# The halves of a PSUM bank added by one reduction on VectorE, without ScalarE's copy

## What is computed

```python
h = rmsnorm(x, g_mix);  z = h @ w_in             # gates, conv inputs, q, k, v
conv_branch = (cb * causal_dwconv(cc * cv, conv_w)) @ w_conv_out
attn_branch = forgetting_attention(q, k, v, log_f) @ w_attn_out
x = x + (sigmoid(gate_c) * conv_branch + sigmoid(gate_a) * attn_branch) @ w_mix_out
x = x + square(relu(rmsnorm(x, g_mlp) @ w_ff1)) @ w_ff2          # width 8192
x = rmsnorm(x, g_final)
mod = silu(c) @ w_ada + b_ada                                     # second block
# attention and a state-space mixer on (norm(x) * (1 + scale) + shift) @ w_in_2
x = x + gate1 * (mixed @ w_out)
u = causal_dwconv(norm(x) @ w_up)                                 # width 2 * 5632
x = x + gate2 * ((silu(u_g) * u_v) @ w_down)
out = rms_norm(x, final_norm_g)
```

## Time and profile before

| | us |
|---|---|
| median of three runs (lowest, highest) | 2615.51 (2613.37, 2620.49) |
| the profiled execution, its own time | 2620.42 |
| its span, first to last instruction | 2618.6 |
| TensorE busy (mean granted clock 0.989) | 2549.9 |
| VectorE busy | 2032.7 |
| ScalarE busy | 1324.8 |

### The profile page before, as it was taken

How to read it: one execution, slowest core, us unless ns; L and a number is a source line. 1 busy time by engine, 2 the same in 40 slices (tenths; PEclk the granted TensorE clock), 3 DMA queues, 4 the chain that set the end, 5 groups by cost and what they waited for, 6 DMA issues and landing times.

```text
span 2618.6 us, 47653 instructions
## 1 busy us (share of the span) xinstructions
PE 2549.9 (97%) x14448; PEld 2211.2 (84%) x14448; DVE 2032.7 (78%) x3152; ACT 1324.8 (51%) x2048; POOL 5.2 (0%) x13
## 2 busy tenths in 40 slices
PE   8999999999999999999998999989899999999998
PEld 7888888888888888888887888868788888888886
DVE  7778775589887887887888558676888888888888
ACT  5444434565554454544554347544545545545456
POOL 0000000000000000000000000000000000000000
PEclk9999999999999999999999999999999999999999
DMA  7786873557888888888885554415455656556554
GB/s 278 258 278 205 269 246 132 182 184 258 278 282 278 279 283 281 279 283 278 281 279 189 175 174 155 138 55 184 146 189 171 200 181 182 191 176 192 191 164 157
DMA packets 160688, 561.95 MB, mean 215 GB/s; under 512 B 18131, under 2 KB 18428, under 8 KB 160636
## 3 DMA queue, kind: packets, MB, share of 16 engines
q1 hardware_dynamic: 132428, 459.04, 52.9%
q10 hardware_dynamic: 27792, 101.20, 12.0%
q0 software_dynamic: 416, 1.06, 0.2%
HBM read 559.12 MB, written 2.11 MB: 214 GB/s over the span
## 4 chain that ended last, share of the span: by engine, by line
PE 94%; DVE 3%; ACT 1%; issue 1%; DMA 1%; DVEq 0%; ACTq 0%; SPq 0%
PE bank L284 94%; DVE w_lo L973 1%; ACT w_hi L573 0%; DMA w_raw<-in_w_gate 0%; DVE R L1006 0%; PE bank L424 0%; DMA X<-in_x 0%; DVE Z L1056 0%; PE bank L415 0%; DVE ss L1423 0%; DVE Z L1577 0%; DVE G L1460 0%; DVE H L1438 0%; ACT scratch L592 0%; ACT bank L599 0%
## 5 line engine op out<-in xcount | busy, mean ns | idle before, releaser
L284 PE MATMUL bank<-H,w_hi 128*128 128x512 f32 (+1 forms) x4736 | 1658.9, 396 | 25.4 <-DVE w_lo L1024 9.9
L284 PE MATMUL bank<-H,w_lo 128*128 128x256 f32 x4672 | 1314.1, 282 | 0.0
L973 DVE TENSOR_TENSOR w_lo<-w_raw,w_hi 128x1024 fp32r<-128x1024 f32 x900 | 1092.2, 1222 | 144.4 <-ACT w_hi L573 136.2
L284 PEld LDWEIGHTS bank<-H,w_hi 128*128 128x128 f32 x4736 | 892.1, 189 | 234.0 <-issue 17.9
L573 ACT ACTIVATE w_hi<-w_raw 128x1024 fp32r<-128x1024 f32 x900 | 910.6, 1051 | 2.9 <-DMA w_raw<-in_w_gate 2.6
L284 PEld LDWEIGHTS bank<-H,w_lo 128*128 128x128 f32 x4672 | 889.5, 190 | 0.1
L284 PE MATMUL bank<-U,w_hi 128*128 128x512 f32 x1984 | 700.5, 397 | 5.5 <-DVE U L1558 4.9
L284 PE MATMUL bank<-U,w_lo 128*128 128x256 f32 x1984 | 558.0, 281 | 0.0
L592 ACT ACTIVATE scratch<-bank 128x256 f32<-128x256 f32 x356 | 136.8, 384 | 825.6 <-PE bank L284 825.5
L284 PEld LDWEIGHTS bank<-U,w_hi 128*128 128x128 f32 x1984 | 372.4, 188 | 98.0 <-DVE U L1558 6.2
L284 PEld LDWEIGHTS bank<-U,w_lo 128*128 128x128 f32 x1984 | 373.9, 188 | 0.0
(11 more groups left out here) (198 smaller groups left out, 1157.6 us busy)
## 6 DMA issues: line engine op xcount, KB each, us to landing
w_raw<-in_w_ff SPq DMA_DIRECT2D x256, 512.0 KB, 4.9
ada_w<-in_w_ada ACTq DMA_DIRECT2D x192, 512.0 KB, 4.6
w_raw<-in_w_up SPq DMA_DIRECT2D x176, 512.0 KB, 4.1
w_raw<-in_w_z SPq DMA_DIRECT2D x96, 512.0 KB, 4.8
w_raw<-in_w_in SPq DMA_DIRECT2D x88, 512.0 KB, 3.9
w_raw<-in_w_gate SPq DMA_DIRECT2D x64, 512.0 KB, 4.6
w_raw<-in_w_down SPq DMA_DIRECT2D x64, 384.0 KB, 3.1
w_raw<-in_w_down SPq DMA_DIRECT2D x64, 320.0 KB, 3.4
```

Of the source, the lines that this page charges most:

```text
L284: return nc.tensor.matmul(out, lhsT, rhs, start=start, stop=stop, skip_group_check=True)
L973: TT(w_lo[:, slot, :], w_raw[:, slot, :], w_hi[:, slot, :].bitcast(F32), ALU.subtract)\
```

## The change

A unit's sum is one `tensor_reduce` on VectorE that reads the whole bank as 256 groups of two, each group a column of the lower half and the column 256 further on, and adds each group. ScalarE's copies, their waits and `halves`, `halves_b`, `half` and `half2` are gone. VectorE waits for `piece_used` itself. In all units that have a `split_low` of slot 0, it now stands ahead of the sum on VectorE; `cast_high` of slot 0 comes first on ScalarE, where the copy was. In out2 and down the gate is applied in the instruction that adds to X. All other instructions are as before.

```diff
-            def take_half(pair, par, scale=1.0):
-
-                act.wait_ge(sem("piece_used"), CREDIT + 4 * pair + 2 * par + 2)
-                A(half[par], bank[par][:, T:2 * T], ACT.Copy, scale=scale).then_inc(sem("halves"), 1)
...
-            def add_halves(pair, par, out):
-
-                dve.wait_ge(sem("halves"), units_with_half(pair, par))
-                TT(out, bank[par][:, 0:T], half[par], ALU.add).then_inc(sem("bank_read"), 1)
+            def add_halves(pair, par, out, first=0):
+
+                dve.wait_ge(sem("piece_used"), CREDIT + 4 * pair + 2 * par + 2)
+                return v.tensor_reduce(out, bank[first + par][:, :].rearrange("p (a t) -> p t a", a=2), AX_X, ALU.add)
+
+            def add_unit(pair, par, out):
+
+                add_halves(pair, par, out).then_inc(sem("bank_read"), 1)
                 return 2 + 2 * pair + par + 1
...
                     pair, m = PAIR0["branch"] + i, 2 * i + par
-                    dve.wait_ge(sem("halves_b"), 2 * m + 2)
-                    TT(total[par], bank[par][:, 0:T], half[par], ALU.add).then_inc(sem("branch.sum"), 1)
-                    TT(conv[par], bank[2 + par][:, 0:T], half2[par], ALU.add).then_inc(sem("bank_read"), 1)
                     split_low(pair + 1, par, 0)
+                    add_halves(pair, par, total[par]).then_inc(sem("branch.sum"), 1)
+                    add_halves(pair, par, conv[par], 2).then_inc(sem("bank_read"), 1)
...
                         add_ada(ADA0["ff"] + 32 * g + u, int(g > 0), par)
-                        n = add_halves(pair + i, par, total[par])
+                        split_low(pair + i + 1, par, 0)
+                        n = add_unit(pair + i, par, total[par])
                         dve.wait_ge(sem("bank_read"), n)
 
                         STT(wide[par], total[par], 0.0, R[:, :], ALU.max, ALU.mult).then_inc(sem("ff.relu"), 1)
-                        split_low(pair + i + 1, par, 0)
                         dve.wait_ge(sem("ff.u_full"), m + 1)
                         TT(ob(U, u, 1), conv[par], ob(U, u, 0).bitcast(F32), ALU.subtract).then_inc(sem("ff.u_ready"), 1)
                         split_low(pair + i + 1, par, 1)
...
-                dve.wait_ge(sem("halves"), units_with_half(pair, par))
-                STT(total[par], bank[par][:, 0:T], mod[:, bass.ds(gate + block, 1)], half[par], ALU.mult, ALU.add)\
-                    .then_inc(sem("bank_read"), 1)
...
+                n = add_unit(pair, par, total[par])
+                dve.wait_ge(sem("bank_read"), n)
+                STT(xb(block), total[par], mod[:, bass.ds(gate + block, 1)], xb(block), ALU.mult, ALU.add)\
+                    .then_inc(sem(name + ".x"), 1)
...
-                    n = add_halves(pair + i, 0, total[0])
                     split_low(pair + i + 1, 0, 0)
+                    n = add_unit(pair + i, 0, total[0])
...
-                    n = add_halves(pair + i, 1, total[1])
+                    split_low(pair + i + 1, 1, 0)
+                    n = add_unit(pair + i, 1, total[1])
                     ffn_conv(pair + i, 1, m + 1, n)
                     dve.wait_ge(sem("up.silu"), j + 1)
                     dve.wait_ge(sem("up.conv"), m + 2)
                     TT(wide[0], wide[1], conv[1], ALU.mult).then_inc(sem("up.act"), 1)
-                    split_low(pair + i + 1, 1, 0)
```

More of the change, by code:

```diff
@@ L796, in ff2_unit @@
             def ff2_unit(pair, par, m, block, chunk, squares=False, last=False):
-                if last:
-                    cast_high(pair + 1, par, 0)
-                take_half(pair, par)
+                cast_high(pair + 1, par, 0)
                 if not last:
-                    cast_high(pair + 1, par, 0)
                     cast_high(pair + 1, par, 1)
@@ L900, in gated_unit @@
             def gated_unit(name, pair, par, m, block, gate, squares, ahead=True, last=False):
-                if last:
+                if ahead:
                     cast_high(pair + 1, par, 0)
-                take_half(pair, par, scale=mod[:, bass.ds(gate + block, 1)])
                 if ahead and not last:
-                    cast_high(pair + 1, par, 0)
                     cast_high(pair + 1, par, 1)
@@ L1047, in raw_unit @@
             def raw_unit(pair, par):
-                add_halves(PAIR0["gate"] + pair, par, flat(G[:, pair:pair + 1, par, :]))
                 split_low(PAIR0["gate"] + pair + 1, par, 0)
+                add_unit(PAIR0["gate"] + pair, par, flat(G[:, pair:pair + 1, par, :]))
                 split_low(PAIR0["gate"] + pair + 1, par, 1)
@@ L1119, in _ @@
                     pair, m = PAIR0["conv_mul"] + i, 2 * i + par
-                    n = add_halves(pair, par, total[par])
                     split_low(pair + 1, par, 0)
+                    n = add_unit(pair, par, total[par])
                     dve.wait_ge(sem("bank_read"), n)
@@ L1281, in second @@
                     add_ada(ADA0["ff"] + 32 * g + 16 + u, int(g > 0), par)
-                    if last:
-                        split_low(pair + 8 + i + 1, par, 0)
-                    n = add_halves(pair + 8 + i, par, total[par])
-                    if not final:
-                        split_low(pair + 8 + i + 1, par, 0)
+                    split_low(pair + 8 + i + 1, par, 0)
+                    n = add_unit(pair + 8 + i, par, total[par])
                     dve.wait_ge(sem("bank_read"), n)
                     TT(xb(u), xb(u), total[par], ALU.add).then_inc(sem("ff.x"), 1)
-                    if final and not last:
-                        split_low(pair + 8 + i + 1, par, 0)
                     if not last:
@@ L1336, in plain_unit @@
             def plain_unit(pair, par, block):
-                dve.wait_ge(sem("halves"), units_with_half(pair, par))
-                TT(zb(block), bank[par][:, 0:T], half[par], ALU.add).then_inc(sem("bank_read"), 1)
                 split_low(pair + 1, par, 0)
+                add_unit(pair, par, zb(block))
                 split_low(pair + 1, par, 1)
@@ L1496, in gated @@
             def gated(name, pair, par, m, block, gate, squares, ahead=True, last=False):
-                if last:
+                if ahead:
                     split_low(pair + 1, par, 0)
-                dve.wait_ge(sem("halves"), units_with_half(pair, par))
-                STT(total[par], bank[par][:, 0:T], mod[:, bass.ds(gate + block, 1)], half[par], ALU.mult, ALU.add)\
-                    .then_inc(sem("bank_read"), 1)
-                if ahead and not squares:
-                    split_low(pair + 1, par, 0)
-                dve.wait_ge(sem("bank_read"), 2 + 2 * pair + par + 1)
-                TT(xb(block), xb(block), total[par], ALU.add).then_inc(sem(name + ".x"), 1)
-                if ahead and squares and not last:
-                    split_low(pair + 1, par, 0)
+                n = add_unit(pair, par, total[par])
+                dve.wait_ge(sem("bank_read"), n)
+                STT(xb(block), total[par], mod[:, bass.ds(gate + block, 1)], xb(block), ALU.mult, ALU.add)\
+                    .then_inc(sem(name + ".x"), 1)
                 if ahead and not last:
```

20 lines of the change are left out of this document (2 added, 18 removed).

## The result

The changed kernel takes **2714.97 us** (median of 4 runs, 2712.43 to 2716.67) beside 2617.86 us of the kernel before (4 runs, 2613.37 to 2620.49): ratio 1.0368, 95% interval 1.0354 to 1.0383. The forecast was 2702 us, with a range of 2672 to 2805. The profiled execution took 2712.4 us, its span 2710.4, which is 91.8 us more than the span before.

What follows compares the result with a forecast made beforehand. The prediction took TensorE, 94% of the chain of waits, to bound the kernel before. Its terms 48 (ff1, ff2) + 31 (up, down) + 6 (branch) + 2 (rest) = +87 on the median 2615.5 gave 2702 us, range 2672 to 2805.

Steps and rivals of the forecast that it cites:

- R: Length of the new sum on VectorE, taken as 0.68 us, 0.26 us more than the old add of 0.42.
- the bounds: For the new sum's length: 0.68 us from bank rows read in order, 1.03 us from an SBUF reduction that jumps 1 KB.
- The term of +48 for ff1 and ff2: ff1, 64 units: 6.49 us against 5.54, 15.2 us per group of 16, of which ff2 returns 3.2; four groups.
- together 11.91 against 11.10: up, 44 pairs: new pair of 5.09 plus 6.82 us against the old, 8.8 us per group; +31 us with down's return.
- About 1 us per group comes back in down: down: VectorE's loop of 3.5 us is below TensorE's 3.8, so it returns about 1 us of up's loss per group.
- rival 2: ff1: TensorE's clock falls as it idles; half of 64 units at 1.2 GHz, +140, about 2840 us; chance 0.04.
- ScalarE is in the loop, since the first split precedes the sums: branch, 16 units: the split needs ScalarE's cast, behind two sigmoids; 6.1 us against some 5.65, +6 us.
- The rest: Other stages: mostly hidden by TensorE, mix included; +1 each for the start and the state-space part, +2 in the sum.
- removed copies give nothing: ScalarE's removed copies, 137 us in the largest group, save nothing, as they ran while TensorE worked.
- 1: Rival: the sum's jump costs in the bank as in SBUF, R = 1.03; 2786 us; chance 0.32.
- 4: Rival: not slower, VectorE's loops stay below 5.54 and 11.10 us and only stage ends show; 2613 us; chance 0.04.
- The predicted chain: Chain of waits, as a sign: VectorE and ScalarE with some 40% where they had 4%.

Runs made afterwards that it cites:

- experiment 4: Changed kernel with each sum over neighbouring columns instead of columns 256 apart, plus ten short sums at the end: 2724.81 us.
- experiment 1: Changed kernel with every first split back behind its sum, the new sum kept: 2612.64 us, 0.9973 of the kernel before.
- experiment 2: Changed kernel with the old order of splits in ff1 alone: 2662.72 us.
- experiment 5: Changed kernel with the old order of splits in up alone: 2672.11 us, 1.0203 of the kernel before.
- experiment 6: Changed kernel with the old order everywhere but in ff1 and up: 2704.46 us, 1.0326 of the kernel before.
- experiment 3: Kernel before, copies and add kept, with the change's order in ff1 alone (first split before sum, first cast before copy): 2654.0 us beside 2619.78.
- experiment 7: Experiment 1's kernel with each sum of ff1 and up done twice, first into a spare buffer: 2653.73 us.

## Why the prediction was right

**R.** Predicted 0.68, measured 0.686. The choice between the bounds (the memory of the nearest rows, against the access of the other) was right; experiment 4 shows that even the number of rows would have been enough reason.

**ff1.** Predicted 6.49 per unit, seen 6.42; predicted wait for the square about 0.9, seen 1.09. Experiments 1 and 2 remove it by the order alone, with the sum kept. In the kernel before, the split filled the square's time, and that cover was what the change gave up. The term of +48 for ff1 and ff2 came out at +47.9, but by luck: both its parts were 4 us too large. ff1's is 0.07 us per unit (the working's own parts add to 6.51). ff2 returned 8.8 and not 12.8, though 1.6 of the 8.8 is a shorter pitch of TensorE in its first group; the last section shows what kept it low.

**up.** The step "together 11.91 against 11.10" was mis-sized: 12.13. The second unit is the predicted one (6.82), the first took 5.31 instead of 5.09. There the first tap starts 0.37 us after the sum's end, where 0.19 was taken from the other unit; that is 0.18 of the 0.22, and why the same dependence takes two lengths was not found. Over 44 pairs the changed kernel is 10.8 us above the working (534.9 against 524.0). The difference to before grew by 4.4 less, since two of that kernel's four groups ran at 11.3 per pair and not at 11.1.

**down.** "About 1 us per group comes back in down, whose loop of R + 2.85 = 3.5 is below TensorE's 11 x 0.35 = 3.8" did not come true: the first three groups returned 0.4 us in all, though the loop was sized nearly right. Timeline of VectorE in experiment 5, at the start of the second down group:

```profile
2217.65 0.68 DVE L959 TENSOR_REDUCE scratch<-bank 128x256 f32<-128x512 f32 x1
...
2219.01 2.35 DVE L953 TENSOR_TENSOR w_lo<-w_raw,w_hi 128x1024 fp32r<-128x1024 f32 x2
2221.28 0.68 DVE L959 TENSOR_REDUCE scratch<-bank 128x256 f32<-128x512 f32 x1
```

The sums are 3.63 us apart, and no split waits. VectorE and ScalarE in the changed kernel's second group:

```profile
2251.01 0.68 DVE L959 TENSOR_REDUCE scratch<-bank 128x256 f32<-128x512 f32 x1
...
2252.67 1.06 ACT L571 ACTIVATE w_hi<-w_raw 128x1024 fp32r<-128x1024 f32 x1 [1.06 <-PE bank L282]
2253.77 1.23 DVE L953 TENSOR_TENSOR w_lo<-w_raw,w_hi 128x1024 fp32r<-128x1024 f32 x1 [0.19 <-ACT w_hi L571]
2254.91 0.68 DVE L959 TENSOR_REDUCE scratch<-bank 128x256 f32<-128x512 f32 x1
```

The 3.90 us from sum to sum are TensorE's pace and not VectorE's: the split waits for its cast, the cast for TensorE, and TensorE's 11 chunks follow one another at 0.353 us, 3.89 per unit, with no idle time. So VectorE has nothing left to catch up with. What differs is the start of the group. TensorE first waits for the last low part of U, 3.9 us in the changed kernel and 1.05 in experiment 5. The 3 us right behind the wait (TensorE's busy time is the second number, the granted clock the third from the end), first in the changed kernel, then in experiment 5:

```profile
2237.00:2240.00 3.00, 3.00 (x10) 2.58 (x11) 2.78 (x3) 2.08 (x3) 0.00 (x0) 0.52 0.16 22
```

```profile
2216.00:2219.00 3.00, 3.00 (x19) 2.59 (x19) 2.73 (x4) 1.86 (x3) 0.00 (x0) 1.00 0.74 208
```

The changed kernel has 10 matmuls in them at a granted clock of 0.52, experiment 5 has 19 at 1.00. From the first sum of a group to its last, where a chunk takes 0.353 us, the changed kernel takes 58.2 and 58.4 us, and experiment 5 57.1; 15 units at TensorE's pace are 58.3. The 1.2 us are thus returned where the clock stays up, and not where it falls. The step that failed is that the sum took TensorE's clock as unchanged at the starts of stages; rival 2 looked for its fall in ff1 alone.

The last group's squares were no part of the prediction at all: the wait for ScalarE that was found in branch occurs there too, at 14 units, and costs 5.6 us to the group's last sum (experiment 6 takes 5.2 of them away). The rule "ScalarE is in the loop, since the first split precedes the sums" was applied in one place and not looked for in every stage.

**branch.** +6 predicted, +6.7 seen, and gone in experiment 6. The working itself gives a little more than its result: 6.1 against 5.65 for 16 units is 7.2. Units were 6.0 us apart, in most of the stage.

**The rest.** +2 predicted, -10.2 seen. mix was hidden, as forecast (91.3 us before and after; its R + 4.8 is 5.48, not 5.45). conv_mul costs 4.4, where 2.4 was forecast (0.3 for 8 units), and v returns 2.6 of it; experiment 6 shows it to be the order's too. The gain is in qk (-4.6), in2 (-3.8) and z (-5.1, after +1.7 in in2_conv). Part of it comes with the copies' removal; "removed copies give nothing" was too strong. With the old order in the stage and TensorE's chunks at 0.353 us, qk took 99.6 and 99.4 us with the copies (before, experiment 3) and 97.2 to 97.6 without (experiments 1, 6, 7), in2 142.9 with and 141.2 without (experiments 3 and 7, the granted clock at 1.00 in both), z 103.1 with and 101.5 without (experiments 3 and 1). That is some 5.5 us; in qk the granted clock is part of it (0.97 with the copies, 0.98 without). The rest goes with TensorE's clock and pitch, which differ by execution: in2 took 145.6 in the kernel before at a clock of 0.98 and 142.9 in experiment 3 at 1.00, both with the copies. Which of TensorE's waits got shorter was not followed.

**The sum.** +87 was forecast, and the traces differ by 91.8. That it is so close is in part luck: up and down cost 7 and 9 us more than forecast, and the 12 us by which the rest came out lower offset most of that.

**The rivals.** 1 fell with experiment 4. 2 did not come in ff1, where the granted clock stayed 1.00 up to TensorE's wait for ff2, but in small at the starts of ff2 and down, where it cost the returns above. 4 fell: the wait behind the relu grew instead of being absorbed. The predicted chain (40% for VectorE and ScalarE) reads 28%, with another 10% as "issue" that the prediction had not named. TensorE's busy time was to stay near 2550 and reads 2585.9: its matmuls' ends are modelled, and some ran at the lower clock. How much is owed to which was not separated.

## What to carry to other kernels

When an edit moves an instruction, ask first what it was hiding where it stood: here a 1.2 us split that hid another engine's square together with a sum longer by 0.26 us cost 57 us in one stage, and the longer sum alone nothing that shows. Then look in every stage, not only in the one that shows it, for what the moved instruction now needs earlier, since an engine's other work in program order may stand ahead of it. In-order engines that feed each other need the filler between the hand-over and its answer; the version with one instruction for the sum and the old order takes 0.9973 of the time before. And where a slower engine makes TensorE wait at the start of a stage, reckon with its clock: here the fall behind the wait took back what the next stage should have returned.

## What was not expected of the hardware

**The clock after one short wait.** At each start of ff2, TensorE waits some 2.4 us for the last low part of U. Stretches (TensorE's busy time is the second number, the granted clock the third from the end) of the third group's start, first in the changed kernel, then in its second trace:

```profile
1175.30:1178.30 3.00, 0.67 (x3) 0.60 (x4) 1.54 (x4) 2.13 (x4) 0.00 (x0) 1.00 0.79 247
1178.30:1181.30 3.00, 3.00 (x11) 2.58 (x10) 3.00 (x5) 1.49 (x2) 0.00 (x0) 0.51 0.77 281
1181.30:1184.30 3.00, 3.00 (x17) 2.58 (x17) 2.86 (x5) 1.06 (x1) 0.00 (x0) 0.92 0.77 261
```

```profile
1178.00:1181.00 3.00, 0.62 (x3) 0.58 (x4) 1.55 (x4) 2.09 (x4) 0.00 (x0) 1.00 0.77 213
1181.00:1184.00 3.00, 3.00 (x18) 2.58 (x18) 3.00 (x4) 1.48 (x2) 0.00 (x0) 1.00 0.81 277
```

The same code and the same wait: once the clock is at its lower level (0.51, that is 1.2 GHz for nearly all of the 3 us), once it stays at the upper. With the fall, ff2 returns 1.1 of the time that ff1 lost, without it 2.7 (90.4 - 89.3 and 90.4 - 87.7 us), where 3.2 were predicted. All starts of ff2 and down in the ten traces, by how long TensorE stands idle there for the last low part of U:

| TensorE's wait | starts | the clock fell in |
|---|---|---|
| none | ff2 of the kernel before, experiments 1 and 2 | 0 of 12 |
| 0.9 to 1.3 us | ff2 of experiment 7, down of the kernel before, experiments 1, 3 and 5 | 0 of 20 |
| 2.1 to 2.7 us | ff2 of the changed kernel (both traces), experiments 3, 4, 5 and 6, down of experiment 7 | 20 of 28 |
| 3.8 to 3.9 us | down of the changed kernel (both traces), experiments 2, 4 and 6 | 20 of 20 |

So a lead that is built up in one stage may be lost on TensorE's clock in the next. Its price shows where the wait and the pitch are the same. Of down groups with a wait of 3.9 us and chunks at 0.353 us, those with a granted clock of 0.81 to 0.84 over the 9 us behind the wait took 58.1 to 58.4 us from the first sum to the last, and those with 0.68 to 0.70 took 59.2 to 59.6 (changed kernel, its second trace, experiment 4). That the fall follows from the wait is a reading of these traces: experiments 2 and 5, which shortened it (to nothing in ff2, to 1.05 us in down), changed the order of the splits too.

**Two pitches of TensorE.** Where nothing waits, a unit of 16 chunks takes 5.55 or 5.65 us (0.347 or 0.353 us per chunk), mostly one value for a whole stage, at a granted clock of 1.00 in both. In two traces of the same kernel the third group of ff2 has 5.65 both times, the first 5.55 once and 5.65 once. One stage of 16 units can so differ by 1.6 us between executions, and differences per stage of that size prove nothing. mix varies more than that (91.30 and 95.34 us in the same two traces); it had the shorter pitch and a granted clock of 1.00 in the first, the longer and 0.99 in the second, which leaves a part of the 4 us. The cause of the two pitches and of that part is open.
